# Low halves of the gate tiles on VectorE instead of GpSimd in the mixing stages of a two-block transformer

## The reference, cut to what matters

```python
def _mixer_merge(p, ml_out, ..., w_branch, w_out):
    branches = (ml_out,
                _gmlp_branch(p[..., GM_OFF:CV_OFF], gm_ln_g, gm_ln_b, gm_w_s, gm_b_s),
                _conv_branch(p[..., CV_OFF:FT_OFF], cv_dw_w, cv_dw_b, cv_ln_g, cv_ln_b),
                _fourier_branch(p[..., FT_OFF:GATE_OFF]))
    y = None
    for i, z in enumerate(branches):
        gate = jax.nn.sigmoid(p[..., GATE_OFF + i * D_MODEL:GATE_OFF + (i + 1) * D_MODEL])
        term = gate * (z @ w_branch[i])
        y = term if y is None else y + term
    return y @ w_out
```

## Time and profile before

| | us |
|---|---|
| median of three runs | 4461.1 |
| the profiled execution, its own time | 4468.33 |
| its span | 4466.5 |
| TensorE busy | 4192.1 (94% of the span) |
| VectorE busy | 2558.6 (57%) |
| ScalarE busy | 1695.9 (38%) |
| GpSimd busy | 460.9 (10%) |

### The profile page before, as it was taken

One profiled execution on the slowest core, in us unless ns is written; L12 is line 12 of the kernel. 1 busy time (PEld: TensorE's weight loads), 2 busy tenths in 40 slices (PEclk: granted clock), 3 DMA queues, 4 the chain that ended last, 5 costly groups with the idle time before them and its releaser, 6 DMA issues. The chain is left out here.

```text
span 4466.5 us, 63337 instructions
## 1 busy us (share of the span) xinstructions
PE 4192.1 (94%) x25846; PEld 3663.0 (82%) x25846; DVE 2558.6 (57%) x5184; ACT 1695.9 (38%) x2136; POOL 460.9 (10%) x130
## 2 busy tenths in 40 slices
PE   7999899999999999999889899999998988897898
PEld 5877788888887888888778789998887977887697
DVE  5635578766641344444484588755665745653664
ACT  3433233333333322222245445444444423433453
POOL 2322034100000000000044250000000021000000
PEclk8999999999999999999899999999999988998999
DMA  6421224455558655555444456687886401545164
GB/s 246 134 89 60 100 89 143 128 176 187 188 207 304 226 192 189 196 198 190 147 128 128 147 172 208 233 314 260 290 283 225 143 8 58 175 142 168 60 192 137
DMA packets 456715, 766.13 MB, mean 172 GB/s; under 512 B 20453, under 2 KB 332965, under 8 KB 436169
## 3 DMA queue, kind: packets, MB, share of 16 engines
q1 hardware_dynamic: 456426, 762.08, 51.2%
HBM read 658.64 MB, written 103.37 MB: 171 GB/s over the span
## 5 line engine op out<-in xcount | busy, mean ns | idle before, releaser
L113 PE MATMUL bank<-hThi_l,pr_whi 128*128 128x512 f32 (+1 forms) x2304 | 788.1, 342 | 19.8 <-POOL pr_wlo L1885 13.0
L113 PE MATMUL bank<-hTlo_l,pr_whi 128*128 128x512 f32 (+1 forms) x2304 | 778.3, 338 | 0.0
L113 PE MATMUL bank<-hThi_l,pr_wlo 128*128 128x512 f32 (+1 forms) x2304 | 777.9, 338 | 0.0
L1997 ACT ACTIVATE pr_whi<-pr_w 128x2048 fp32r<-128x2048 f32 x270 | 515.5, 1909 | 239.7 <-DMA pr_w<-peer_v_in 237.2
L113 PE MATMUL bank<-pr_whi,pr_ahi 128*128 128x512 f32 x1536 | 599.0, 390 | 7.5 <-DVE pr_alo L2191 7.4
L113 PE MATMUL bank<-pr_whi,pr_alo 128*128 128x512 f32 x1536 | 598.3, 390 | 0.0
L113 PE MATMUL bank<-pr_wlo,pr_ahi 128*128 128x512 f32 x1536 | 598.3, 390 | 0.0
L113 PEld LDWEIGHTS bank<-hThi_l,pr_whi 128*128 128x128 f32 x2304 | 440.9, 191 | 69.5 <-POOL pr_wlo L1885 14.8
L113 PEld LDWEIGHTS bank<-hThi_l,pr_wlo 128*128 128x128 f32 x2304 | 440.6, 191 | 45.7
L113 PEld LDWEIGHTS bank<-hTlo_l,pr_whi 128*128 128x128 f32 x2304 | 441.2, 191 | 43.2
L2177 DVE TENSOR_TENSOR pr_a<-pr_gs,pr_g 128x1024 f32<-128x1024 f32 (+1 forms) x128 | 122.7, 959 | 486.3 <-DMA pr_g<-dense_weights 486.3
(11 more groups left out here) (592 smaller groups left out, 8417.7 us busy)
## 6 DMA issues: line engine op xcount, KB each, us to landing
pr_w<-peer_u_in SPq DMA_DIRECT2D x128, 1024.0 KB, 5.7
pr_w<-peer_v_in SPq DMA_DIRECT2D x128, 1024.0 KB, 5.0
dense_weights<-pr_buf SPq DMA_DIRECT2D x12, 4096.0 KB, 16.8
gu_w<-ffn_w_up_in SPq DMA_DIRECT2D x88, 512.0 KB, 4.7
gr_w<-w_in_in SPq DMA_DIRECT2D x32, 1024.0 KB, 5.3
expert_scores<-pr_s SPq DMA_DIRECT2D x64, 512.0 KB, 6.8
pr_gs<-expert_scores SPq DMA_DIRECT2D x64, 512.0 KB, 5.9
pr_g<-dense_weights SPq DMA_DIRECT2D x64, 512.0 KB, 7.1
```

The costliest lines, as they stand in the source:

```text
L113: ins = pe.matmul(psum, a, b, start=first and i == 0, stop=last and i == len(terms) - 1)
L1997: act.activation(w_hi[:, n % slots, :, :], wt[:, n % ring, :, :], ACT.Copy).then_inc(hi_ready, 1)
```

## The change

The loop of GpSimd goes, and VectorE makes the low halves in a new function `split_lo(n)` with the same instruction and the same wait for the high half. Its fifteen calls stand at fixed places of VectorE's row: tile 1 behind `statistics(0)`, tile 2 behind `statistics(1)` and so ahead of `gate_rows`, tile 3 inside `gate_rows` between the first scans and L1506, tile 4 between `gate_rows` and `normalise(0)`, and tiles 5 to 15 at even i of the loop, behind `take_branch(i - 8)`. In ScalarE's row `split_hi(1)` moves from the loop's first turn to the front of the row, ahead of the three activations on the gates.

```diff
-            @block.gpsimd
-            def _(pool):
-                for n in range(1, n_w):
-                    pool.wait_ge(hi_ready, n + 1 - first)
-                    pool.tensor_tensor(w_lo[:, held.slot(n), :, :], wt[:, held.slot(n), :, :], w_hi[:, n % slots, :, :].bitcast(F32),
-                                       ALU.subtract).then_inc(lo_ready, 1)
...
+                split_hi(1)
                 act.wait_ge(gates_biased, 1)
...
                 for i in range(halves_n):
-                    if i % 2 == 0 and i // 2 + 1 < n_w:
+                    if i % 2 == 0 and 1 < i // 2 + 1 < n_w:
                         split_hi(i // 2 + 1)
...
                     chain(last)
+                    split_lo(3)
                     chain(dve.tensor_tensor(li_r[:, :, :], li_r[:, :, :], cum[:, :, :], ALU.subtract))
...
+                def split_lo(n):
+                    dve.wait_ge(hi_ready, n + 1 - first)
+                    dve.tensor_tensor(w_lo[:, held.slot(n), :, :], wt[:, held.slot(n), :, :], w_hi[:, n % slots, :, :].bitcast(F32),
+                                      ALU.subtract).then_inc(lo_ready, 1)
...
                 statistics(0, v_rows, gm_stat)
+                split_lo(1)
                 dve.wait_ge(softened, 3)
...
                 statistics(1, cv_rows, cv_stat)
+                split_lo(2)
                 gate_rows()
+                split_lo(4)
                 dve.wait_ge(gm_in, 64)
                 dve.wait_ge(gm_root, 1)
                 normalise(0, v_rows, ln, gm_normed)
...
                     take_branch(i - 8)
+                    if i % 2 == 0 and i // 2 + 1 < n_w:
+                        split_lo(i // 2 + 1)
```

## The result

The changed kernel takes 4485.03 us, the median of four runs (4479.05 to 4491.25), against 4460.33 us of the kernel before in the same runs (4456.37 to 4465.73): a ratio of 1.0051, 95% interval 1.0039 to 1.0064, so slower. A second set with more rounds gave 4478.31 against 4463.15 us, 1.0038 (1.0025 to 1.0051); of this set one run of each kernel, 5337.49 and 14543.7 us, was a slow one and is left out here and in all that follows (with them the medians are 4479.31 and 4463.48 us). The forecast was 17.0 us more (0.38%); the two sets have 24.7 and 15.2 us. The profiled execution took 4479.05 us with a span of 4477.3 us, the lowest of its set.

The account below looks back on a forecast made before the run. TensorE, busy 94% of the span, was taken as the bound. Layer 0's 1.3 + 10.1 + 2.2 - 1.9 = 11.7 us plus layer 1's 5.3 made 17.0 us, giving 4478.1 us on the 4461.1 median; range 4466 to 4488.

Parts of the forecast that it names:

- Tile 4 in layer 0: VectorE's low half ahead of `normalise(0)` waits for gate half 5's successor on ScalarE; TensorE stalls 10.1 us before `fourier_channels(1)`.
- Tile 2: Low half ahead of `gate_rows` delays the sixteen copies: TensorE stalls 1.3 us in layer 0; `fourier_time(0)` 2.7 us later in layer 1.
- The clock: TensorE's lower clock after layer 0's 10.1 us stall: 2.2 us lost, bounds 0 and 4.4; in layer 1, 1.0 us.
- a low clock for longer than 5 us behind the wait: Sign that the prediction is wrong: TensorE's clock stays low over 5 us after L1258's second group, in layer 0.
- Gate half 8 in layer 1: Delays through tiles 3 and 4 make `normalise(1)`, hence gate half 8, 6.0 us late, 5.0 to 7.2 by the clock.
- What GpSimd's end frees: VectorE instructions no longer held: TensorE wins 1.9 us in layer 0, 0.7 us in layer 1; loop's eleven low halves cost nothing.
- The sum: Both mixing stages together: 11.7 us more in layer 0 and 5.3 us in layer 1, 17.0 us in all.
- the one by which VectorE's release decides: Both stages: only the held instructions count, so the kernel gets faster, at most 6.6 us, 4454 to 4458; 5 in 100.

## Why the prediction was right, point by point

The mechanism, the places and most sizes held; two sizes were off and cancelled (points 3 and 4).

1. *Tile 4 in layer 0*: forecast 10.1 us ahead of `fourier_channels(1)`, measured 10.01 us, and 10.0 in every version that kept the call there; moving the one call took it away.
2. *Tile 2*: forecast 1.3 us in layer 0, measured 1.43 and 2.1 us (with the load of tile 2); in layer 1 forecast 2.7 us later than before, measured from the stage's first matmul 20.2 - 17.3 = 2.9 us.
3. *The clock*: forecast 2.2 us behind the long wait. From that wait's end to `turn_back_gates` five profiles with it took 9.2 to 10.4 us, where the kernel before took 7.4: 1.8 to 3.0 us. One of the prediction's signs of being wrong did come up, a low clock for longer than 5 us behind the wait: 6.1 us here and 5.8 in one version. Its price, 3.0 us, stayed inside the bound of 4.4. In layer 1 I took 1.0 us and it was 6.38 - 3.99 = 2.4 us. I had reckoned with 5.9 us of idle time; it was 7.1 us, as gate half 2 now ran wholly at the upper level and ended sooner.
4. *Gate half 8 in layer 1*: forecast 6.0 us later with 7.2 as the upper bound; from the stage's first matmul it was 52.4 - 45.0 = 7.4 us, the clock's 1.4 us more and just over the bound. The stage as a whole lost 5.0 us (forecast 5.3), so 2.4 us were won back behind it instead of 0.7. That the stage's sum met the forecast is luck: the two errors cancel. The 2.9 us wait ahead of `turn_back_gates` (L1261), which the prediction didn't name, is a part of the same lateness: TensorE now stands there, and less at gate half 8.
5. *What GpSimd's end frees*: no low half on VectorE took over 2.29 us, no addition L1553 over 0.70 us, and the two waits of layer 0 for a sigmoid are gone, as forecast. The eleven low halves of the loop cost nothing that shows. In layer 0 the time behind `turn_back_gates`, less TensorE's waits there and less what the lower granted clock took, is 243.8 to 244.8 us in all twelve profiles, with the low halves on either engine.
6. *The sum*: the two profiles of the changed kernel have both stages together 14.7 and 18.4 us longer than the first profile of before, 17.3 and 21.0 us longer than the second, and the two sets of runs 24.7 and 15.2 us; the forecast was 17.0. Layer 0 up to `turn_back_gates` lost 14.9 and 16.1 us where the terms give 1.3 + 10.1 + 2.2 = 13.6; behind it 5.1 and 1.9 us were given back against the first profile of before, forecast 1.9, and the granted clock there, 0.979 and 0.967, makes nearly all of that difference. So a nearness of 2 us is partly chance. That the first set came out 8 us higher was not brought to a cause. The bounds of the terms, added up, give 13 to 23 us and not 13 to 21.

Of the rivals, the one by which VectorE's release decides was right in its own term and wrong in its condition. With the same fifteen low halves a stage on VectorE, and the three dear waits moved, the kernel is 10.9 us faster than before. So what the forecast took as a small gain, 1.9 + 0.7 us, is larger in layer 1, because there VectorE's row leads to gate half 8, and three instructions of that row were held for 2.6, 4.4 and 4.4 us. Of layer 1's gain, 3 to 6 us went with the move in ScalarE's row; how much of the rest is the release of the three and how much the granted clock wasn't separated.

## What to carry to other kernels

When work moves into another engine's row, its wait moves with it: ask what the input's producer needs before it can run, and put the call behind everything that the next engine wants earlier than that. Here three calls in other places of the same row made 26 us, while the work itself cost nothing that shows. A wait is costed from the event it hangs on, not by its own length: VectorE's longest ones (9.6 us in layer 0, 10.6 us in layer 1) were nearly free to keep, since the next wait ended last.

## What the runs showed of the hardware

A VectorE instruction can be held by GpSimd even when it is small: a bias over 128x64 took 3.76 instead of 0.23 us, and a `tensor_scalar` with one tensor input 5.44 us for its four instead of 1.38. Both lay under a GpSimd `tensor_tensor` of 4.5 to 4.6 us that had begun first. Even two `tensor_scalar` instructions over 4x256 took 4.87 instead of 0.48 us.

TensorE's granted clock was 0.50 for the first 3.4 to 6.1 us behind a wait of 10 to 12 us in the middle of full work (five profiles), and eight matmuls there took 3.75 instead of 1.89 us; the price of the stall, 1.8 to 3.0 us, differed between executions of the same kernel (3.0 and 1.9 us for the changed one). Apart from it, unchanged code outside the two stages differed by 6 us between the four profiles of the table and by 10 us between all twelve, as much as the effects of single calls here, so that these are read from the stages and the waits.
